# Five tiles of a hybrid attention and recurrence layer turned by VectorE and two DMA passes, in place of TensorE

## The chip, the cores and the metric

The kernel runs on one core of one Trainium2 chip. The metric is the device time of one execution in microseconds (us), the median of several runs. A core has TensorE (PE in the profile; PEld is its weight load), VectorE (DVE), ScalarE (ACT), GpSimd (POOL) and SyncE (SP). Each runs its own instructions in the order in which they were written, and they wait for one another through counting semaphores. The tensors that the engines work on lie in SBUF (128 partitions) or PSUM, the weights and the input in DRAM.

## What is computed

One layer on 256 tokens of width 2048, everything in float32:

```python
h = RMSNorm(x)
hq, hf, hi, hg, c_q, c_kv, k_r = split(h @ w_in)       # 4 x 1024, 512, 512, 64 columns
# head group A: gated linear recurrence, 8 heads of 128, run in two groups (g = 0, 1) of 4 heads
#   f = lb + (1 - lb) * sigmoid(hf);  S_t = diag(f_t) S_{t-1} + (1 - f_t) hi_t^T;  o_t = S_t^T silu(hq_t)
#   o_A = RMSNorm(o) * silu(hg)
# head group B: latent attention, 8 heads
#   q = RMSNorm(c_q) @ w_uq;  k, v = RMSNorm(c_kv) @ w_ukv;  RMSNorm per head, rotary part, softmax
x = x + concat(o_A, o_B) @ w_out
x = x + (silu(g) * u) @ w_down,   g, u = RMSNorm(x) @ w_gate_up
```

## The kernel before, in words

**Products.** Every weight product runs in float32 by parts: a weight tile is split into `w_hi` (ACT, line 757) and `w_lo` (DVE, line 1084), the activations likewise into a `_hi` and a `_lo` tile, and PE adds three products (lines 1693 and 1696). The activations are PE's stationary operand and must stand with the width on the partitions, so each of them is turned (tokens from the partitions to the free axis) before its product.

**Granules.** The first half of the kernel, up to about 430 us, is a row of 137 granules of two weight tiles (128 x 1024 where a block is 512 wide). The blocks stand in this order: `lat` 0 to 2 (the latents `c_q`, `c_kv` and the rotary key), then `hq0 uq0 hf0 ukv0 hi0 uq1 hg0 ukv1 hq1 uq2 ukv2 hf1 uq3 ukv3 hi1 hg1`, then `out1` and `out2`. A block from `w_in` has 8 granules, one from `w_uq` or `w_ukv` has 2. ACT and DVE convert three granules ahead of PE, through a ring of four slots: conversion n waits until PE has used granule n - 4.

**Steps.** Everything else is a step with a place in `SCHEDULE`, which the function `schedule` writes: a granule number and a name. Each engine, in its loop over the granules, first converts (ACT, DVE) or first does its steps and then multiplies (PE). All engines take the steps of a granule in the same order, and no engine passes over one that waits. A conversion that stands behind a waiting or a long step waits with it.

**Turning.** A tile is turned by PE: 8 matmuls of 128 x 128 against `ident`, into a ring of four PSUM banks (`side`), from where ACT and DVE read it. This is so for the normed latents (`lat_t`, `turn_x`, line 1716), the recurrence's queries (`turn` with n = 0, line 1794) and gates (`turn` with n = 1), and the recurrence's output (`o_t`, line 1716). From the feed-forward part on (after 470 us) the kernel has a second way for its hidden tile: DVE turns every 32 x 32 block (line 1475, STREAM_TRANSPOSE), POOL sends the tile to DRAM (line 712) and fetches it back in four pieces in which the blocks have changed places (line 718).

**The steps that the prediction follows.** `q_t` (line 1751) turns the attention's queries, which the step `q_b` makes on DVE (lines 1252 and 1135 to 1140). `lev_b` (lines 1338 and 1339) makes the tiles that `pairs` (line 1805) multiplies. `q_b` also frees the PSUM bank that the block after next needs: the block `hi1` waits for `q_b` of `uq3`.

Of the kernel before, what the change touches and what calls it, by code (L numbers as in the profile page):

```python
# [31 lines left out]
P = 128  # L32
# [182 lines left out]
def schedule():  # L215
# [32 lines left out]
    for g in range(2):  # L248
# [3 lines left out]
        s += [(e + 2 + 2 * g + n * (1 + g), ("turn", g, n, t)) for n in range(2) for t in range(NT)]  # L252
# [10 lines left out]
        s += [(p, ("o_a", g)), (p + 1, ("o_b", g))]  # L263
# [33 lines left out]
def side_uses(step):  # L297

    kind = step[0]
    if kind in ("x", "x2", "lat_t", "o_t"):  # L300
        return [(step, "dve")]
    if kind in ("vec", "turn", "probs_t", "join7", "join8"):
# [24 lines left out]
SPLIT = {step: n for n, step in enumerate(SPLITS)}  # L327

# [31 lines left out]
def hybrid_layer(nc, x, positions, attn_norm_w, w_in, hgrn_lb, hgrn_norm_w, mla_q_norm_w, w_uq, mla_kv_norm_w,  # L360
# [7 lines left out]
    with ExitStack() as ctx:  # L368
# [34 lines left out]
        def mb(name, shape, dt=F32):  # L403
            return sb(name, shape, dt, mix)
# [24 lines left out]
        more_rows = stage[0:V_ROWS - KT, 0, 0, 1, 0:P]  # L429
        keep = mb("keep", [P, SEQ])  # L430
# [15 lines left out]
        latents = (lat, hv)  # L446
        qTn = X[:, 0, :].rearrange("p (h t) -> p h t", h=HEADS)
# [9 lines left out]
        squares = nc.dram_tensor("squares", (P // Q, Q, P // Q, SEQ), F32, kind="Internal").ap()  # L457
        first_two = sb("first_two", [P, WIDE])
# [7 lines left out]
        corner, partly, both = gate[:, 0, :], gate[:, 1, :], hidden[:, 0, :]  # L466

# [45 lines left out]

        s_turned = sem("s_turned")
# [132 lines left out]
        def _(pool):  # L647
# [100 lines left out]
        def _(act):  # L748
# [48 lines left out]

            def split_hi(parts):
# [8 lines left out]
            def step(s):  # L807
# [30 lines left out]
                elif kind == "lat_t":  # L838
                    i, j = a
                    ps, k, col = filled(s), 4 * i + 2 * j, (V_KVN if i else V_QN) + 2 * j  # L840
                    split_hi([(mT_hi[:, k + n, :], ps[:, n * SEQ:(n + 1) * SEQ], col + n) for n in range(2)])
# [46 lines left out]
                elif kind in ("hq", "hf_a", "hi", "hg"):  # L888
# [3 lines left out]
                    if kind == "hq" and not a[0]:  # L892
                        act.wait_ge(s_side, USE[("lat_t", 0, 1)] + 1)
                    if a[0] and kind == "hg":
                        act.wait_ge(s_given["dve"], GIVEN[USE[("o_a", 0, NT - 1)]])
# [3 lines left out]
                elif kind == "turn":  # L899
# [45 lines left out]
                elif kind == "o_t":  # L945
                    g, j = a
                    dst, k = (hT_hi, 12 + 2 * j) if g else (mT_hi, MT[HEADS + 2 * j])
                    split_hi([(dst[:, k:k + 2, :], filled(s)[:, :].rearrange("p (k t) -> p k t", k=2), V_HG)])
# [122 lines left out]
        def _(dve):  # L1071
# [26 lines left out]
            def split_lo(s, parts):  # L1098
# [73 lines left out]
            def step(s):  # L1172
# [33 lines left out]
                elif kind == "lat_t":  # L1206
                    i, j = a
                    ps, k, col = filled(s), 4 * i + 2 * j, (V_KVN if i else V_QN) + 2 * j
                    split_lo(s, [(mT_lo[:, k + n, :], ps[:, n * SEQ:(n + 1) * SEQ], mT_hi[:, k + n, :], col + n)
                                 for n in range(2)])  # L1210
# [98 lines left out]
                elif kind == "lev_a":  # L1309
# [97 lines left out]
                elif kind == "o_t":  # L1407
                    g, j = a
                    hi, lo, k = (hT_hi, hT_lo, 12 + 2 * j) if g else (mT_hi, mT_lo, MT[HEADS + 2 * j])
                    split_lo(s, [(lo[:, k:k + 2, :], filled(s)[:, :].rearrange("p (k t) -> p k t", k=2),  # L1410
                                  hi[:, k:k + 2, :], V_HG)])
# [267 lines left out]
        def _(pe):  # L1679
# [39 lines left out]
            def step(s):  # L1719
# [20 lines left out]
                elif kind == "lat_t":  # L1740
                    i, j = a
                    pe.wait_ge(s_lat, NT * (i + 1))
                    turn_x(s, 2 * j, latents[i])
# [40 lines left out]
                elif kind == "turn":  # L1784
                    g, n, t = a
                    if n == 0:
                        b = BLOCK_OF[("hq", g)]
                        pe.wait_ge(s_taken[b % 2], taken(b))
                    else:
                        pe.wait_ge(s_lbused, g + 1)  # L1790
                    ps = use(s)
                    for h in range(GH):
                        cols = slice(h * P, (h + 1) * P)
                        m = transpose(ps[:, cols], (hq, hlf)[n][:, t, cols], ident[:, :])
# [56 lines left out]
                elif kind == "o_t":  # L1851
# [181 lines left out]
```

## Time and profile before

| | us |
|---|---|
| median of 3 runs | 1124.82 (1124.74 to 1125.54) |
| the profiled execution | 1124.67 |
| its span in the profile | 1122.9 |

The difference between the last two, 1.8 us, lies around the span. The profile gives the busy time of each engine, the waits (who waited for whom), the groups of like instructions, and a timeline, in which each row has the start and the duration of an instruction or of several equal ones in a row, and, in brackets, how long its engine had been idle before it and who ended that. Durations overlap: an engine starts the next instruction before the last one is fully written.

### The profile page before, as it was taken

Reading aid. Unit: us, or ns where it says so; the run is one execution under the profiler, and the core shown is the slowest. Engines: PE = TensorE matmul, PEld = TensorE weight load, DVE = VectorE, ACT = ScalarE, POOL = GpSimd, SP = SyncE. Lnnn points to the kernel's source line nnn. Section 1 sums busy time; section 2 is a strip of 40 time slices with the busy share of each in tenths; the row PEclk is TensorE's granted clock in tenths of the full one; section 3 lists DMA queues with packets and bytes.
Section 4 is the critical chain, followed back from the end, with each engine's and each line's share of the span. In section 5 each row is a group of like instructions: output and inputs, shape, how many; then the busy total and the mean of one; then the engine's idle time right before and its main releaser. Section 6 shows DMA issues by size and latency. Waiting matters only on the chain.

```text
span 1122.9 us, 15465 instructions
## 1 busy us (share of the span) xinstructions
PE 1113.2 (99%) x5265; PEld 937.8 (84%) x5265; DVE 886.8 (79%) x1198; ACT 640.5 (57%) x907; POOL 51.1 (5%) x134
## 2 busy tenths in 40 slices
PE   7999999999999999999999999999999999999998
PEld 7988888888888888888888888888888888888887
DVE  5578786587876667688888888888988879889777
ACT  7566776668664556454554554554554555555553
POOL 3000000000000000000000000000000010000000
PEclk9999999999999999999999999999999999999999
DMA  8666455545555455667777677777777686666655
GB/s 267 192 196 189 158 159 156 164 141 170 197 177 168 153 187 169 212 212 234 225 229 237 222 232 238 222 229 236 224 235 226 224 276 217 207 206 199 211 190 169
DMA packets 107239, 228.99 MB, mean 204 GB/s; under 512 B 8201, under 2 KB 19250, under 8 KB 106930
## 3 DMA queue, kind: packets, MB, share of 16 engines
q1 hardware_dynamic: 101346, 209.30, 58.9%
q0 software_dynamic: 5536, 18.88, 5.8%
q8 instruction: 29, 0.48, 0.2%
q14 instruction: 24, 0.20, 0.0%
q10 hardware_dynamic: 304, 0.14, 0.0%
HBM read 218.32 MB, written 9.96 MB: 203 GB/s over the span
## 4 chain that ended last, share of the span: by engine, by line
PE 97%; DVE 2%; DMA 1%; ACT 0%; issue 0%; SPq 0%; DVEq 0%; ACTq 0%
PE side L1919 25%; PE main L1693 22%; PE side L1921 12%; PE main L1696 11%; PE side L1891 4%; PE side L1892 4%; PE side L1893 4%; PE main L1893 3%; PE main L1891 3%; PE main L1892 3%; PE side L1817 1%; PE side L1716 1%; DMA raw<-in_w_in 1%; PE side L1764 0%; PE side L1765 0%; DVE w_lo L1084 0%
## 5 line engine op out<-in xcount | busy, mean ns | idle before, releaser
L977 ACT CAST w_hi<-raw 128x1024 fp32r<-128x1024 f32 (+1 forms) x245 | 241.6, 990 | 172.2 <-PE side L1919 104.9
L1532 DVE TENSOR_TENSOR w_lo<-raw,w_hi 128x1024 fp32r<-128x1024 f32 (+1 forms) x245 | 275.4, 1139 | 21.9 <-ACT w_hi L977 21.6
L1084 DVE TENSOR_TENSOR w_lo<-raw,w_hi 128x1024 fp32r<-128x1024 f32 (+3 forms) x156 | 178.5, 1154 | 107.9 <-ACT w_hi L757 105.6
L757 ACT CAST w_hi<-raw 128x1024 fp32r<-128x1024 f32 (+3 forms) x156 | 153.7, 993 | 142.5 <-PE main L1693 137.6
L1693 PE MATMUL main<-w_hi,hT_hi 128*128 128x512 f32 (+2 forms) x448 | 173.4, 388 | 1.7 <-DVE hT_lo L1105 1.4
L1696 PE MATMUL main<-w_hi,hT_lo 128*128 128x512 f32 (+2 forms) x448 | 169.1, 378 | 0.0
L1921 PE MATMUL side<-w_hi,hT_lo 128*128 128x512 f32 x400 | 155.6, 389 | 0.0
L1919 PE MATMUL side<-w_hi,hT_hi 128*128 128x512 f32 x400 | 155.6, 389 | 0.0
L1693 PE MATMUL main<-w_lo,hT_hi 128*128 128x512 f32 (+2 forms) x448 | 114.6, 377 | 0.0
L1919 PE MATMUL side<-w_lo,hT_hi 128*128 128x512 f32 x400 | 106.9, 389 | 0.0
L1693 PEld LDWEIGHTS main<-w_hi,hT_hi 128*128 128x128 f32 x448 | 84.7, 189 | 15.5 <-DVE hT_lo L1105 1.8
L1696 PEld LDWEIGHTS main<-w_hi,hT_lo 128*128 128x128 f32 x448 | 84.8, 189 | 13.0
L1693 PEld LDWEIGHTS main<-w_lo,hT_hi 128*128 128x128 f32 x448 | 82.9, 189 | 14.1
L1919 PEld LDWEIGHTS side<-w_hi,hT_hi 128*128 128x128 f32 x400 | 75.1, 188 | 15.6
L1919 PEld LDWEIGHTS side<-w_lo,hT_hi 128*128 128x128 f32 x400 | 75.1, 188 | 15.6
L1921 PEld LDWEIGHTS side<-w_hi,hT_lo 128*128 128x128 f32 x400 | 75.1, 188 | 15.5
L1921 PE MATMUL side<-w_hi,aT_lo 128*128 128x512 f32 x208 | 80.9, 389 | 0.0
L1919 PE MATMUL side<-w_hi,aT_hi 128*128 128x512 f32 x208 | 80.9, 389 | 0.0
L1532 DVE TENSOR_TENSOR w_lo<-last_two,w_hi 128x1024 fp32r<-128x1024 f32 x36 | 44.1, 1225 | 43.5 <-ACT w_hi L977 43.5
L977 ACT CAST w_hi<-last_two 128x1024 fp32r<-128x1024 f32 x36 | 37.9, 1052 | 59.9 <-PE side L1919 59.9
L977 ACT CAST w_hi<-first_two 128x1024 fp32r<-128x1024 f32 x36 | 38.0, 1056 | 58.4 <-PE side L1919 58.4
L1693 PE MATMUL main<-w_hi,mT_hi 128*128 128x512 f32 (+1 forms) x160 | 62.0, 387 | 0.0
(279 smaller groups left out, 1819.0 us busy)
## 6 DMA issues: line engine op xcount, KB each, us to landing
raw<-in_w_gate_up SPq DMA_DIRECT2D x176, 512.0 KB, 4.8
raw<-in_w_down SPq DMA_DIRECT2D x88, 512.0 KB, 4.5
raw<-in_w_in SPq DMA_DIRECT2D x64, 512.0 KB, 3.8
raw<-in_w_out SPq DMA_DIRECT2D x32, 512.0 KB, 3.7
raw<-in_w_in SPq DMA_DIRECT2D x15, 384.0 KB, 4.5
squares<-hiddenT POOLq DMA_DIRECT2D x11, 512.0 KB, 5.0
hiddenT<-squares POOLq DMA_DIRECT2D x44, 128.0 KB, 5.3
raw<-in_w_ukv SPq DMA_DIRECT2D x8, 512.0 KB, 3.9
```

What stands on the lines that cost most here:

```text
L757: copy(w_hi[:, slot, 0:n], raw[:, slot, 0:n]).then_inc(s_hi, 1)
L977: copy(w_hi[:, n % RING, 0:cols], src).then_inc(s_hi, 1)
L1084: tt(w_lo[:, slot, 0:n], raw[:, slot, 0:n], w_hi[:, slot, 0:n].bitcast(F32), ALU.subtract)\
L1532: tt(w_lo[:, n % RING, 0:cols], src, w_hi[:, n % RING, 0:cols].bitcast(F32), ALU.subtract)\
L1693: m = matmul(banks[t][:, 0:cols], hi[:, at[n], tok], rhs, start=(part == "hi" and k == k_first), stop=(part == "lo" and k == last))
L1696: matmul(banks[t][:, 0:cols], lo[:, at[n], tok], rhs, start=False, stop=False)
L1716: m = transpose(ps[:, at:at + P], where[:, t, (k + n) * P:(k + n + 1) * P], ident[:, :])
L1891: matmul(bank, hi, big, start=first, stop=False)
L1892: matmul(bank, lo, big, start=False, stop=False)
L1893: return matmul(bank, hi, small, start=False, stop=last)
L1919: m = matmul(bank, hi, rhs, start=False, stop=(part == "lo" and (t, half) in last))
L1921: matmul(bank, lo, rhs, start=False, stop=False)
```

## The change

Five tiles are turned in the way of the hidden tile: the two normed latents (`lat` 0 and 1), the queries of both recurrence groups (`hq` 0 and 1), and the output of the first group (`o` 0). The gates and the second group's output stay with PE. A new step `swap` does the DVE part, and POOL the moves:

```diff
+            def swap(key, src):                                   # on DVE
+                nc.vector.transpose(swap_of[key].rearrange("p b (n r) -> p n b r", r=Q),
+                                    src.rearrange("p t (k b c) -> p (t k) b c", b=P // Q, c=Q)).then_inc(s_swap, 1)
...
+            def swap(*key):                                       # on POOL
+                n, at = SWAP[key], swap_of[key]
+                pool.wait_ge(s_swap, n + 1)
+                pool.dma_start(swapped[n].rearrange("a c b x -> (a c) b x"), at).then_inc(s_parked, 16)
+                pool.wait_ge(s_parked, 16 * (n + 1))
+                for b in range(P // Q):
+                    pool.dma_start(at[Q * b:Q * (b + 1), :, :], swapped[n, :, :, b, :].rearrange("a c x -> c a x"))\
+                        .then_inc(s_landed, 16)
```

The places in the schedule, and the order on POOL:

```diff
-        s += [(e + 1, ("lat_a", i)), (e + 2, ("lat_b", i))] + [(e + 5, ("lat_t", i, n)) for n in range(2)]
+        s += [(e + 1, ("lat_a", i)), (e + 2, ("lat_b", i)), (e + 2, ("swap", "lat", i))]
+        s += [(e + 13 - 2 * i + n, ("lat_t", i, n)) for n in range(2)]
...
-        s += [(e + 2 + 2 * g + n * (1 + g), ("turn", g, n, t)) for n in range(2) for t in range(NT)]
+        s += [(END[("hq", g)] + 1, ("swap", "hq", g))]
+        s += [(e + 2 - 4 * g, ("turn", g, 0, t)) for t in range(NT)] + [(e + 3 + 3 * g, ("turn", g, 1, t)) for t in range(NT)]
...
-        s += [(p, ("o_a", g)), (p + 1, ("o_b", g))]
+        s += [(p, ("o_a", g)), (p + 1, ("o_b", g))] + [(p + 1, ("swap", "o", g))] * (g == 0)
...
+            swap("lat", 0)
+            swap("lat", 1)
+            swap("hq", 0)
             pool.wait_ge(s_lbused, 1)
             pool.wait_ge(s_side, USE[("join8", 0)] + 1)
             pool.dma_start(lb[:, :, :], hgrn_lb[:, GW:2 * GW].partition_broadcast(P)).then_inc(s_lbin, 16)
+            swap("hq", 1)
+
+            swap("o", 0)
```

ACT and DVE then read the turned tile from SBUF, ACT after a wait for its landing. DVE's split of a latent becomes 4 instructions of 128 x 128 per half in place of 2 of 128 x 256, that of the output 8 of 128 x 128 in place of 2 of 128 x 512:

```diff
-                    ps, k, col = filled(s), 4 * i + 2 * j, (V_KVN if i else V_QN) + 2 * j
-                    split_hi([(mT_hi[:, k + n, :], ps[:, n * SEQ:(n + 1) * SEQ], col + n) for n in range(2)])
+                    k, col = 4 * i + 2 * j, (V_KVN if i else V_QN) + 2 * j
+                    landed("lat", i)
+                    split_hi([(by_quarter(mT_hi[:, k + n, :]), swapped_tile(("lat", i), 2 * j + n), col + n)
+                              for n in range(2)])
```

In granules: `swap` of the latents stands at 19 and 27, their splits at 30, 31 and 36, 37 (before at 22 and 30); `swap` of `hq` at 34 and 74, ACT's copies at 45 and 83 (before at 45 and 89); `swap` of `o` at 81, its split at 95 as before. The swaps write into tiles that are free at the time (`hbT`, `hkT`, half of `E`, the new `hq_turned`, `hgate`).

On PE, between the blocks `ukv0` and `hi0` (line 1693 before is line 1766 now), the rows before:

```order
L1693 MATMUL main<-w_lo,mT_hi 128x512 x4
L1794 MATMUL side<-ident,lat 128x128 x8
L1693 MATMUL main<-w_hi,hT_hi 128x512
L1696 MATMUL main<-w_hi,hT_lo 128x512
L1693 MATMUL main<-w_hi,hT_hi 128x512
```

and now:

```order
L1766 MATMUL main<-w_lo,mT_hi 128x512 x4
L1766 MATMUL main<-w_hi,hT_hi 128x512
L1769 MATMUL main<-w_hi,hT_lo 128x512
L1766 MATMUL main<-w_hi,hT_hi 128x512
L1769 MATMUL main<-w_hi,hT_lo 128x512
```

The 8 matmuls that turned the queries (their tile bears the name `lat`, whose memory it shares) are gone, and the granules on both sides stand next to each other.

On DVE, in front of `q_t` of the first head pair (`stage_r` is what `q_t` turns, `krw` and `kr` the rotary key), the rows before:

```order
L1140 TENSOR_TENSOR kr<-rot 128x2x32
L1084 TENSOR_TENSOR w_lo<-raw,w_hi 128x1024
L1236 TENSOR_SCALAR stat<-stat 128x4
L1084 TENSOR_TENSOR w_lo<-raw,w_hi 128x1024
L1123 TENSOR_TENSOR stat<-stat 128x4
L1124 SCALAR_TENSOR_TENSOR stat<-stat 128x4
```

and now:

```order
L1195 TENSOR_TENSOR kr<-rot 128x2x32
L1164 STREAM_TRANSPOSE E<-lat 128x8x4x32
L1134 TENSOR_TENSOR w_lo<-raw,w_hi 128x1024
L1303 TENSOR_SCALAR stat<-stat 128x4
L1134 TENSOR_TENSOR w_lo<-raw,w_hi 128x1024
L1155 SCALAR_TENSOR_TENSOR mT_lo<-hkT,vec_cols,mT_hi 128x128 x4
L1178 TENSOR_TENSOR stat<-stat 128x4
L1179 SCALAR_TENSOR_TENSOR stat<-stat 128x4
```

A block turn and four small splits have moved in between the rotary key and the work on the queries.

On DVE, behind `q_b` of the third head pair, the rows before:

```order
L1139 TENSOR_TENSOR stage_r<-rot 128x128
L1140 TENSOR_TENSOR stage_r<-rot 128x128
L1084 TENSOR_TENSOR w_lo<-raw,w_hi 128x1024
L1103 TENSOR_TENSOR mT_lo<-side,mT_hi 128x256
L1084 TENSOR_TENSOR w_lo<-raw,w_hi 128x1024
```

and now:

```order
L1194 TENSOR_TENSOR stage_r<-rot 128x4x32
L1195 TENSOR_TENSOR stage_r<-rot 128x4x32
L1164 STREAM_TRANSPOSE hq_turned<-lat 128x8x4x32
L1134 TENSOR_TENSOR w_lo<-raw,w_hi 128x1024
L1153 TENSOR_TENSOR mT_lo<-side,mT_hi 128x256
L1134 TENSOR_TENSOR w_lo<-raw,w_hi 128x1024
```

The turn of the second group's queries stands ahead of the conversion of granule 78. The fifth turn (`hgate<-E`) stands in the same way directly behind the eight instructions of `o_b` (line 1403) and ahead of the conversion of granule 85.

## Rows read from the trace of the kernel before

**Rows 1.** The page, busy time, share and instructions of each engine.

```profile
PE 1113.2 (99%) x5265; PEld 937.8 (84%) x5265; DVE 886.8 (79%) x1198; ACT 640.5 (57%) x907; POOL 51.1 (5%) x134
```

**Rows 2.** Waits of PE, longest first: total us, times, longest.

```profile
PE side L1730 <- POOL freq L669: 3.0, 1, 3.0
PE main L1693 <- DVE hT_lo L1105: 1.4, 2, 1.0
...
```

**Rows 3.** Timeline of PE at the first latent: start, us, instruction.

```profile
54.89 0.75 PE L1693 MATMUL main<-w_lo,hT_hi 128*128 128x320 f32 x4
55.48 1.03 PE L1716 MATMUL side<-ident,lat 128*128 128x128 f32 x8
56.27 0.39 PE L1693 MATMUL main<-w_hi,hT_hi 128*128 128x320 f32 x1
56.50 0.31 PE L1696 MATMUL main<-w_hi,hT_lo 128*128 128x320 f32 x1
```

**Rows 4.** One tile's instructions, `hiddenT`: ns min/median/max, first and last start.

```profile
L718 POOL DMA_DIRECT2D hiddenT<-squares x44: 551/554/570, 478.6 to 904.3; - x44
...
L1475 DVE STREAM_TRANSPOSE hiddenT<-hidden x11: 1233/1235/1240, 471.3 to 895.1; 128x1024 f32<-128x1024 f32 x11
```

**Rows 5.** Groups of DVE and ACT by shape: busy us, mean ns, idle before.

```profile
L1167 DVE SCALAR_TENSOR_TENSOR sincos<-rot,sincos 128x128 f32<-128x128 f32 x6 | 1.8, 292 | 0.2
...
L804 ACT ACTIVATE mT_hi<-side,vec_cols 128x256 fp32r<-128x256 f32 x8 | 3.1, 474 | 0.0
```

**Rows 6.** The page, DMA issues: KB each, median us to landing.

```profile
squares<-hiddenT POOLq DMA_DIRECT2D x11, 512.0 KB, 5.0
hiddenT<-squares POOLq DMA_DIRECT2D x44, 128.0 KB, 5.3
```

**Rows 7.** Timeline of ACT around granules 34 to 36.

```profile
81.44 1.79 ACT L757 CAST w_hi<-raw 128x768 fp32r<-128x768 f32 x2
84.59 1.06 ACT L757 CAST w_hi<-raw 128x1024 fp32r<-128x1024 f32 x1 [1.35 <-PE main L1693]
```

**Rows 8.** Timeline of DVE and PE in front of the first `q_t`.

```profile
90.62 1.23 DVE L1084 TENSOR_TENSOR w_lo<-raw,w_hi 128x1024 fp32r<-128x1024 f32 x1 [2.78 <-ACT w_hi L757]
...
98.65 0.28 DVE L1140 TENSOR_TENSOR stage_r<-rot 128x128 f32<-128x128 f32 x1
...
99.45 0.60 PE L1751 MATMUL side<-ident,stage 128*128 128x128 f32 x4
```

**Rows 9.** Timeline of ACT, DVE and PE up to the first `pairs`.

```profile
111.27 1.05 ACT L757 CAST w_hi<-raw 128x1024 fp32r<-128x1024 f32 x1 [1.67 <-PE main L1693]
...
138.38 1.22 DVE L1339 TENSOR_TENSOR E<-E,hqT 128x1024 f32<-128x1024 f32 x1
...
139.65 1.05 PE L1805 MATMUL side<-E 128*128 128x128 f32 x7
```

**Rows 10.** Timeline of DVE, ACT and PE from granule 78 to granule 89.

```profile
226.56 1.22 DVE L1084 TENSOR_TENSOR w_lo<-raw,w_hi 128x1024 fp32r<-128x1024 f32 x1
...
229.79 0.21 ACT L790 ACTIVATE stat<-stat 128x4 f32<-128x4 f32 x1 [2.47 <-DVE stat L1114]
...
238.65 1.06 ACT L847 ACTIVATE E<-E 128x1024 f32<-128x1024 f32 x1 [2.23 <-DVE E L1222]
...
246.99 0.35 PE L1764 MATMUL side<-X 128*128 128x128 f32 x1 [0.17 <-DVE E L1403]
...
264.15 1.39 DVE L1252 SCALAR_TENSOR_TENSOR stage<-main,stat,qw_row 128x192 f32<-128x192 f32 x4
...
265.64 0.47 PE L1693 MATMUL main<-w_hi,hT_hi 128*128 128x512 f32 x1
```

**Rows 11.** Timeline of DVE and PE at the second group's first `pairs`.

```profile
298.22 1.23 DVE L1338 TENSOR_TENSOR E<-E,hkT 128x1024 f32<-128x1024 f32 x1 [0.28 <-ACT E L920]
299.36 1.22 DVE L1339 TENSOR_TENSOR E<-E,hqT 128x1024 f32<-128x1024 f32 x1
...
301.52 0.50 PE L1805 MATMUL side<-E 128*128 128x128 f32 x3
```

More of the change, by code:

```diff
@@ L299, in side_uses @@
     kind = step[0]
-    if kind in ("x", "x2", "lat_t", "o_t"):
+    if kind in ("x", "x2") or kind == "o_t" and step[1]:
         return [(step, "dve")]
-    if kind in ("vec", "turn", "probs_t", "join7", "join8"):
+    if kind in ("vec", "probs_t", "join7", "join8") or kind == "turn" and step[2]:
         return [(step, "act")]
@@ L891, in step @@
                                "hg": (hgate, ACT.Silu)}[kind]
-                    if kind == "hq" and not a[0]:
-                        act.wait_ge(s_side, USE[("lat_t", 0, 1)] + 1)
+                    if kind == "hq":
+                        act.wait_ge(s_swap, SWAP[("hq", 0) if a[0] else ("lat", 0)] + 1)
                     if a[0] and kind == "hg":
-                        act.wait_ge(s_given["dve"], GIVEN[USE[("o_a", 0, NT - 1)]])
+                        act.wait_ge(s_tlo, SPLIT[("o_t", 0, 1)] + 1)
                     for t in range(NT):
@@ L946, in step @@
                     g, j = a
-                    dst, k = (hT_hi, 12 + 2 * j) if g else (mT_hi, MT[HEADS + 2 * j])
-                    split_hi([(dst[:, k:k + 2, :], filled(s)[:, :].rearrange("p (k t) -> p k t", k=2), V_HG)])
+                    if not g:
+                        landed("o", g)
+                        split_hi([(by_quarter(mT_hi[:, MT[HEADS + 2 * j + n], :]), swapped_tile(("o", g), 2 * j + n), V_HG)
+                                  for n in range(2)])
+                        return
+                    k = 12 + 2 * j
+                    split_hi([(hT_hi[:, k:k + 2, :], filled(s)[:, :].rearrange("p (k t) -> p k t", k=2), V_HG)])
                 elif kind == "sq2":
@@ L1207, in step @@
                     i, j = a
-                    ps, k, col = filled(s), 4 * i + 2 * j, (V_KVN if i else V_QN) + 2 * j
-                    split_lo(s, [(mT_lo[:, k + n, :], ps[:, n * SEQ:(n + 1) * SEQ], mT_hi[:, k + n, :], col + n)
-                                 for n in range(2)])
+                    k, col = 4 * i + 2 * j, (V_KVN if i else V_QN) + 2 * j
+                    split_lo(s, [(by_quarter(mT_lo[:, k + n, :])[:, t, :, :], swapped_tile(("lat", i), 2 * j + n)[:, t, :, :],
+                                  by_quarter(mT_hi[:, k + n, :])[:, t, :, :], col + n) for n in range(2) for t in range(NT)])
+                elif kind == "swap":
+                    what, i = a
+                    if what == "lat":
+                        dve.wait_ge(s_lat, NT * (i + 1))
+                        swap(a, latents[i][:, :, :])
+                    elif what == "hq":
+                        b = BLOCK_OF[a]
+                        dve.wait_ge(s_taken[b % 2], taken(b))
+                        swap(a, hq[:, :, :])
+                    else:
+                        dve.wait_ge(s_given["dve"], GIVEN[USE[("o_a", i, NT - 1)]])
+                        swap(a, E[:, 0, :].rearrange("p (t c) -> p t c", t=NT))
                 elif kind == "kr_b":
@@ L1739, in step @@
                     turn_x(s, 4 * c + 2 * j)
[L1740 to L1743, printed above, removed]
                 elif kind in ("q_t", "k_t"):
@@ L1783, in step @@
                         .then_inc(s_side, 1)
-                elif kind == "turn":
+                elif kind == "turn" and a[1]:
                     g, n, t = a
[L1786 to L1790, printed above, removed]
+                    pe.wait_ge(s_lbused, g + 1)
                     ps = use(s)
@@ L1850, in step @@
                         m.then_inc(s_side, 1)
-                elif kind == "o_t":
+                elif kind == "o_t" and a[0]:
                     g, j = a
```

45 lines of the change are left out of this document (36 added, 9 removed).

## The prediction

> **What bounds the kernel now.** I read the busy shares first: PE is busy for 99% of the span [rows 1]. Then PE's waits: the two longest items are 3.0 us and 1.4 us, both near the start [rows 2]. So PE's own instructions, one behind the other, are the time, and what leaves PE shortens the kernel unless PE then has to wait. Whether it has to can't be seen in shares. For that I read, in the timeline, every place where PE takes up something that DVE or ACT has made, and how much earlier that was ready. There the kernel is tight: the tile of the first `q_t` was written at 98.65 + 0.28 = 98.93 and PE took it at 99.45, 0.52 us later [rows 8]; the first `pairs` got its tile at 138.38 + 1.22 = 139.60 and began at 139.65 [rows 9]; before granule 89 the bank was free at 264.15 + 1.39 = 265.54 and PE wrote to it at 265.64 [rows 10]; before `scores` of the fifth head PE did wait, 0.17 us for DVE [rows 10]. Nearly every reserve of PE is under 1 us there, so PE, DVE and ACT bound this half together, and DVE's work between two such places is on the path.
>
> **What is removed.** PE loses 5 groups of 8 matmuls. One group: it starts at 55.48 and the next granule at 56.27, 0.79 us; that granule's first matmul is followed after 0.23 us (56.27 to 56.50), where four of the same width take 0.59 from 54.89 to 55.48, 0.15 each, so another 0.08 [rows 3]. That is 0.87 us a group and 4.35 us in all. If nothing else happened, the time would be 1124.67 - 4.35 = 1120.3.
>
> **What is added.** DVE gets 5 block turns of 128x1024, and its like takes 1.235 us [rows 4]. An instruction starts about 0.08 us before its predecessor's end (298.22 + 1.23 = 299.45, the next starts at 299.36) [rows 11], so a turn in an unbroken row costs 1.16; behind a wait for its own engine's last write it costs 1.27. The small splits: 4 of 128x128 per half latent. A like of them takes 0.292 [rows 5], 0.21 in a row, so 0.84 us for four. Bounds: 0.14 each, an eighth of the 1.14 us from start to start of a 128x1024 [rows 11], and 0.29 each with no overlap, so 0.6 to 1.2 us for four; I take 0.21, since the row is of the same size and kind. ACT's copies (0.474 each, 0.39 in a row [rows 5]) stay as many, and I take them at the same cost from SBUF. POOL gets 5 stores and 20 loads; one path is 1.24 (turn) + 5.0 (store landed) + 3 x 0.55 (POOL's issues of the first three loads [rows 4]) + 5.3 (last load landed) [rows 6], about 13.2 us. The time from turn to first reader is about 20 us for the latents (swap at 54, split at 75; swap at 72, split at 92), 27 for `hq` 0, over 20 for `hq` 1, 35 for `o`: hidden, at nothing, and with 6 us to spare each.
>
> A rule of the Trainium skill speaks against moving these turns at all: "VectorE: DVE Perf Modes", section "Rules for kernel authors", says that a 128x128 transpose belongs on TensorE where PSUM will do, and the page's table of transpose paths has 390 ns for one there, in bfloat16. By that figure 40 of them would be worth 15.6 us, an estimate; the trace has 0.11 us each in a row [rows 3], and the sum goes by the trace.
>
> **Where the added work lies, place by place.** At each place PE comes at its own pace or when the chain in front of it ends, whichever is later, so waits inside one chain don't add up; only the last counts.
>
> Place 1, up to the first `q_t` (99.45). Two groups are gone before it, 1.74 us. The chain: conversion 36 on ACT was released by PE at 84.59 [rows 7]; 1.74 earlier would be 82.85. But ACT now has two copies (0.78) between conversions 34 and 35, and what leads up to 34 is the rotary angles and their sine table, which moved by the first group alone: 81.44 - 0.87 = 80.57. The conversions 34 and 35 take 1.79 - 0.08 = 1.71 [rows 7], so 36 starts at 80.57 + 1.71 + 0.78 = 83.06, 1.53 earlier than before. Behind it, through `silu` and two table loads, hangs conversion 37, for which DVE waited 2.78 us at 90.62 [rows 8]; so DVE too is 1.53 earlier there. Then it gets the turn of `hq` 0 (+1.16) and four small splits (+0.84) before `q_b`: ready at 98.93 - 1.53 + 1.16 + 0.84 = 99.40. PE would be there at 97.7. It begins at 99.40 in place of 99.45: of 1.74 us, 0.05 is left. (PE stops once earlier, at `uq0`, whose second split now stands at granule 31, for about 0.65 us; the later wait swallows it.) Bounds by the small splits: -0.25 to +0.35 around this.
>
> Place 2, the first `pairs` (139.65). The third group (at 116) is gone. The chain starts at 111.27, where ACT is released by PE [rows 9], and runs through ACT and DVE without another release by PE to 139.60. It moves with PE's place at 111, not with what leaves PE after it. Reserve 0.05, group 0.87: gained 0.05.
>
> Place 3, granules 78 to 89. The chain begins where the fourth turn goes in, ahead of the conversion at 226.56, hands over from DVE to an idle ACT at 229.79 and 238.65, reaches PE with its 0.17 us wait at 246.99 [rows 10], and goes on over the softmax of the fifth head and the gates of the second group, DVE and ACT in turn, to `q_b` of `uq3`, ready at 265.54. PE releases nothing of it. It gets 1.16 (turn of `hq` 1) + 1.27 (turn of `o`, directly behind `o_b`, whose result it reads) = 2.43 us. PE's reserve at the end is 0.10. So granule 89 starts 2.33 us later than before, counted from the same state at 226, and the fourth group, which stood just ahead of it, is inside that: without its removal PE would have come even later, so its gain is nothing. On the way PE should stop several times, at `scores` (the 0.17 us wait becomes longer) and at `probs_t` of the fifth head.
>
> Place 4, from 266 on. The fifth group (at 288) is gone. The next tight place is `pairs` at 301.52, ready at 299.36 + 1.22 = 300.58: reserve 0.94 [rows 11], just over 0.87. DVE's 8 small splits (1.7) stand where 2 large ones with a stop between them took about as long (estimate). So 0.87 is gained. From there on nothing changes.
>
> Sum: -0.05 - 0.05 + 2.33 - 0.87 = +1.4 us. On the profiled execution 1124.67 + 1.4 = 1126.0; the median of the runs stands 0.15 above that execution, so 1126.2.
>
> **Rivals.** (a) The chains give. If the waits in place 3 were not one chain but had slack in them that a timeline doesn't show, or if ACT and DVE catch up, PE keeps its groups: 1120.3 with all hidden (1120.5 as a median); with place 3 alone at nothing the fourth and fifth group count in full, 1124.67 - 0.1 - 1.74 = 1122.8 (1123.0). For it: DVE is idle for a good part of this half, waiting for ACT's conversions. Against it: the idle time lies ahead of conversions that PE releases, not in these chains. Also in this family, one of the two late turns falls into a gap: 1126.2 - 1.2 = 1125.0.
>
> (b) The moves come late. A transfer would have to be 6 us late to delay ACT's split, which waits in order, with all conversions behind it; PE has about 3 us of converted weights, and from there each further microsecond is one on the time. From 9 us late on this is the bound: a path of 25 us at one latent gives 1126.2 + (25 - 13 - 9) = 1129, at both 1132. For it: POOL's moves here run beside the weight loads and beside a busier DVE. Against: such moves took 5.0 and 5.3 [rows 6], also beside weight loads.
>
> The Trainium skill has a mechanism for it: "SBUF — State Buffer", section "SBUF: two separate sides", says that a DMA issued from GpSimd can be held up while DVE holds their shared port. Here that would be held by w_lo's subtractions, 1.22 us long; 25 issues each held for one of them would put 6 us on a path, which is inside the spare time; no run here has yet shown it for these five.
>
> (c) The small splits and the SBUF copies are dearer than taken. At 0.29 a split place 1 costs 0.35 more, the eight splits in place 4 overdraw the 0.07 reserve by 0.6, and longer turns add a little: 1127.3.
>
> **Numbers.** A measurement of this kernel tells a change of about 0.2%, 2.25 us, from none: faster is below 1122.6, slower above 1127.1. The forecast (1125.3 to 1127.1) has 0.52, a partly hidden place 3 (1122.6 to 1125.3) 0.12, the chains give (a, below 1122.6) 0.12, dearer splits (c, 1127.1 to 1128) 0.14, late moves (b, 1128 to 1132) 0.10. Faster 0.12, same 0.64, slower 0.24. The range leaves out most of (a) and (b): 1122.9 to 1128.2.
>
> **What would show it.** Right: 40 fewer matmuls against `ident`; PE's waits grow from about 6 us by some 5 to 6 us, for DVE, at the first `q_t`, the first `pairs`, `scores`, `probs_t` and granule 89; the first `pairs` starts at nearly its old time, 139.5, and granule 89 near 268. Wrong: granule 89 before 266 (then a), ACT waiting for a DMA at a split (b), or a new wait of PE after 301. A DVE turn far from 1.24 us would move place 3 by twice the difference.

## The result, and the profile after

| | before | after |
|---|---|---|
| median of 7 runs each | 1124.86 (1124.74 to 1125.54) | 1129.26 (1128.92 to 1130.74) |
| the profiled execution | 1124.67 | 1129.12 |
| its span | 1122.9 | 1127.4 |

The ratio after / before is 1.0040, 95% interval 1.0029 to 1.0051: slower by 4.4 us, above the range given. The page's row on busy time answers to [rows 1]:

```profile
PE 1112.1 (99%) x5225; PEld 935.8 (83%) x5225; DVE 894.0 (79%) x1217; ACT 642.0 (57%) x909; POOL 64.8 (6%) x159
```

The 40 matmuls are gone from PE. Its waits, which answer to [rows 2]:

```profile
PE side L1803 <- POOL freq L690: 3.0, 1, 3.0
PE main L1766 <- DVE mT_lo L1155: 2.7, 1, 2.7
PE side L1870 <- DVE E L1406: 1.1, 1, 1.1
PE side L1789 <- DMA X<-in_x: 0.9, 1, 0.9
PE main L1766 <- DVE hT_lo L1155: 0.9, 1, 0.9
PE side L1843 <- DVE probs L1356: 0.8, 1, 0.8
PE main L1766 <- issue: 0.8, 1, 0.8
PE side L1833 <- DVE E L1470: 0.6, 1, 0.6
```

The waits at the first `pairs` (L1870), at `scores` and `probs_t` of the fifth head (L1833, L1843) and before granule 89 ("issue") were forecast. The one of 2.7 us for `mT_lo` was forecast at 0.65 and swallowed. It stands before `uq0`; here is PE's timeline there:

```profile
85.31 0.45 PE L1766 MATMUL main<-w_hi,mT_hi 128*128 128x384 f32 x1 [2.65 <-DVE mT_lo L1155]
85.59 0.34 PE L1769 MATMUL main<-w_hi,mT_lo 128*128 128x384 f32 x1
85.77 0.33 PE L1766 MATMUL main<-w_hi,mT_hi 128*128 128x384 f32 x1
...
88.11 0.53 PE L1766 MATMUL main<-w_hi,mT_hi 128*128 128x384 f32 x1
88.43 0.53 PE L1769 MATMUL main<-w_hi,mT_lo 128*128 128x384 f32 x1
...
102.08 0.60 PE L1820 MATMUL side<-ident,stage 128*128 128x128 f32 x4
```

From 88.11 to 88.43 is 0.32 us, from 85.59 to 85.77 only 0.18: matmuls of the same shape stand nearly twice as far apart for a while. The table by stretches (busy time of PE, PEld, DVE, ACT, POOL, then the granted clock, the DMA share and GB/s) names the reason:

```profile
84.00:86.00 2.00, 0.69 (x4) 0.69 (x5) 2.00 (x6) 1.98 (x4) 0.00 (x0) 1.00 0.67 179
86.00:88.00 2.00, 2.00 (x10) 2.00 (x9) 1.97 (x4) 1.99 (x3) 0.00 (x0) 0.69 0.74 243
88.00:90.00 2.00, 2.00 (x7) 2.00 (x7) 1.45 (x2) 1.97 (x3) 0.00 (x0) 0.50 0.72 240
90.00:92.00 2.00, 2.00 (x11) 1.86 (x11) 1.12 (x1) 1.44 (x2) 0.00 (x0) 0.96 0.63 169
```

Behind the stop the granted clock was 0.50, 1.2 GHz in place of 2.4, for about 3.4 us. Before the stop ACT and DVE had this:

```profile
60.45 1.05 ACT L793 CAST w_hi<-raw 128x1024 fp32r<-128x1024 f32 x1 [1.96 <-DMA raw<-in_w_in]
...
68.82 1.05 ACT L793 CAST w_hi<-raw 128x1024 fp32r<-128x1024 f32 x1 [1.23 <-DMA raw<-in_w_in]
...
75.95 0.16 DVE L1201 CAST pos_f<-pos_i 128x2 f32<-128x2 int32 x1
...
81.50 1.13 DVE L1155 SCALAR_TENSOR_TENSOR mT_lo<-hbT,vec_cols,mT_hi 128x128 fp32r<-128x128 f32 x4
...
84.12 1.13 DVE L1155 SCALAR_TENSOR_TENSOR mT_lo<-hbT,vec_cols,mT_hi 128x128 fp32r<-128x128 f32 x4
...
101.08 0.28 DVE L1195 TENSOR_TENSOR stage_r<-rot 128x128 f32<-128x128 f32 x1
```

ACT waits for weights, which it did not before, and the rotary angles (75.95) begin late. The DMA issues between 54 and 68 us, in the kernel after (first the 512 KB loads of `w_in`, then the moves of latent 0; [rows 6] for their like) and, last, in the kernel before:

```profile
raw<-in_w_in SPq DMA_DIRECT2D x6, 512.0 KB, 6.1
swapped<-hbT POOLq DMA_DIRECT2D x1, 512.0 KB, 3.7
hbT<-swapped POOLq DMA_DIRECT2D x4, 128.0 KB, 6.5
...
raw<-in_w_in SPq DMA_DIRECT2D x6, 512.0 KB, 4.5
```

A weight load took 6.1 us to landing in the median, where it took 4.5.

**Where the time went.** The table gives how much later PE starts a step than in the kernel before, read from the timelines of the profiled executions. The executions differ by up to 1.4 us in their first 14 us (the load of `x`), so the difference at granule 16 (44.24 before) is taken off each. The columns: `uq0` (84.33 before), granule 36 (91.28), first `q_t` (99.45), first `pairs` (139.65), granules 89 (265.64), 95 (288.82) and 152 (465.95). In the kernel after nothing changes from 320 us on. Three other profiled executions lose time behind 500 us, where nothing was edited: lat_on_pe 1.8 us, best_a 0.5, best_b 1.1; in lat_on_pe behind a wait of ACT of 4.18 us for weights, in the others the cause was not sought. So compare the places, not the ends.

| kernel | `uq0` | 36 | `q_t` | `pairs` | 89 | 95 | 152 |
|---|---|---|---|---|---|---|---|
| forecast | | | -0.05 | -0.10 | +2.23 | | +1.4 |
| after | +1.03 | +2.68 | +2.68 | +2.76 | +5.18 | +4.19 | +4.61 |
| after, second profile | +1.01 | +2.68 | +2.68 | +2.74 | +5.15 | +4.15 | +4.62 |
| lat_on_pe | 0.00 | 0.00 | +0.66 | +0.76 | +3.16 | +2.14 | +2.55 |
| lat_alone | +1.00 | +2.65 | +2.65 | +2.67 | +2.72 | +2.68 | +2.68 |
| late_alone | 0.00 | 0.00 | 0.00 | +0.02 | +2.44 | +1.43 | +1.90 |
| no_moves | -0.81 | -0.73 | +0.18 | +0.31 | +2.72 | +1.72 | +2.17 |
| stop_2 | +0.31 | +0.39 | +0.38 | +0.45 | +3.14 | +2.14 | +2.57 |
| stop_3 | +0.89 | +2.57 | +2.57 | +2.65 | +5.09 | +4.08 | +4.51 |
| warm | +1.03 | +1.12 | +2.02 | +2.19 | +4.59 | +3.60 | +4.08 |
| angles_early | -1.79 | -1.79 | -0.07 | +0.06 | +2.72 | +1.71 | +2.16 |
| best_a | -1.78 | -1.78 | -0.14 | +0.39 | +0.42 | -0.56 | -0.46 |
| best_b | -1.78 | -1.76 | -1.77 | -1.75 | -1.70 | -2.69 | -2.58 |
| best_c | -1.78 | +5.67 | +5.67 | +5.70 | +5.75 | +4.76 | +4.85 |

The step from `pairs` to granule 89 is +2.42, forecast +2.33. The step up to `q_t` is +2.68, forecast -0.05: there the forecast failed.

### The profile page after: what moved, and what is told of

Its sections match the earlier page's. It is cut to its first block, busy times and chain, and to the rows that moved or that the text cites. A ratio compares the mean times of both kernels' runs of the same rounds, so it can differ in the third digit from the quotient of the medians.

```text
span 1127.4 us, 15411 instructions
## 1 busy us (share of the span) xinstructions
PE 1112.1 (99%) x5225; PEld 935.8 (83%) x5225; DVE 894.0 (79%) x1217; ACT 642.0 (57%) x909; POOL 64.8 (6%) x159
## 4 chain that ended last, share of the span: by engine, by line
PE 90%; DVE 5%; ACT 2%; DMA 1%; issue 1%; POOL 0%; DVEq 0%; ACTq 0%; POOLq 0%; SPq 0%
PE side L1984 24%; PE main L1766 19%; PE side L1986 12%; PE main L1769 9%; PE side L1956 4%; PE side L1958 4%; PE side L1957 4%; PE main L1958 3%; PE main L1957 3%; PE main L1956 3%; DMA raw<-in_w_in 1%; DVE w_lo L1134 1%; PE side L1882 1%; PE side L1789 1%; ACT w_hi L793 1%
```

## The experiments

The theory: POOL's moves of the first latent compete with the weight loads; ACT's conversions come late, and with them the angles; PE stops long before `uq0`; its clock falls behind the stop. Rivals: each turn costs its 0.9 us wherever it stands; VectorE's work alone does it; the late turns do it.

### Which tiles cost what

A tuple names the tiles that PE turns, as in the kernel before; the others stay as in the kernel after.

```diff
+ON_PE = (('lat', 0), ('lat', 1))                    # lat_on_pe
+ON_PE = (('hq', 0), ('hq', 1), ('o', 0))            # lat_alone
+ON_PE = (('hq', 0), ('lat', 0), ('lat', 1))         # late_alone
```

**lat_on_pe.** 

> The two latents are turned by PE again, at their old granules; the three later tiles stay with VectorE. Theory (the excess over the forecast arises at the latents: weight loads late beside POOL's moves, then a stop of PE of 2.65 us before uq0, then a clock at its lower level for about 3.4 us): no stop before uq0 above 0.3 us, granted clock 1.00 from 84 to 92 us, first q_t 0.6 us later than in the kernel before (turn of hq 0 costs 1.16, reserve 0.52), first pairs 0.6 to 0.7 later, granule 89 about 3.0 later, end 2.3 to 2.6 later: 1127.3 us. Rival (each turn costs its 0.9 us wherever it stands, and the clock is no part of it): the first q_t 1 us or more later, and two fifths of 4.4 us gone, 1127.5, with the clock still falling or the 2.6 us not gone at the first q_t. Rival (the late turns alone make the loss): 1129.

Measured 1127.96 (ratio to the kernel before 1.0026, 1.0016 to 1.0037). No stop before `uq0`, `q_t` +0.66, granule 89 +3.16, granule 152 +2.55: the theory's numbers at each place. Its median is 0.7 over the forecast. Its profiled execution was the slowest of the eight (1130.05), 1.8 us of it lost behind 500 us. The times alone do not tell the theory (1127.3) from the first rival (1127.5); the places do.

**lat_alone.** 

> Only the two latents are turned by VectorE and moved by POOL; hq 0, hq 1 and o 0 are turned by PE as in the kernel before. Theory: the same stop of 2.6 to 2.8 us before uq0, the clock at 0.50 for about 3.4 us behind it, first q_t 2.4 to 2.7 us later than in the kernel before, and nothing given back afterwards, since the chains start from PE: end 2.6 later, 1127.4 us. Rival (a late start at 100 us is absorbed by later reserves, or the late turns are what counts): under 1125.8.

Measured 1127.55 (1.0018, 1.0009 to 1.0027); granule 152 at +2.68 in the profile. The stop (2.63 us), the fall of the clock and the 2.65 us are there with the latents alone, and nothing is given back. The profile shows one sort of execution only: of the eleven runs, seven had a mean granted clock of 0.998 or less and took 1127.3 to 1129.4; the other four had 1.000 and took 1125.7 to 1126.1. Six of the seven had 0.998, with a mean of 1127.7, against 1125.8 for the four: where no later wait swallows it, as here, the fall of the clock costs 1.9 us by the runs, 1.65 by the profile.

**late_alone.** 

> Only hq 1 and o 0 are turned by VectorE. Theory (the step of the forecast on granules 78 to 89 was right): granule 89 starts 2.3 to 2.5 us later than in the kernel before, 0.5 to 0.9 is given back at the group removed before granule 95, end 1.5 to 1.9 later: 1126.5 us. Rival (late turns fall into slack once the first half is undisturbed): granule 89 under 1.3 later, 1125.3 or less.

Measured 1126.86 (1.0016, 1.0007 to 1.0025); granule 89 +2.44, granule 152 +1.90. The forecast's step on granules 78 to 89 holds by itself. 2.68 and 1.90 make 4.58 of the 4.61: the turn of `hq` 0 costs nothing in the kernel after, since PE comes to `q_t` later than its tile is ready.

### The moves, or VectorE's work

POOL passes over both latents, and ACT waits for the turn alone:

```diff
+                if key[0] == "lat":
+                    return
                 pool.wait_ge(s_swap, n + 1)
...
-                act.wait_ge(s_landed, MOVED * (SWAP[key] + 1))
+                if key[0] == "lat":
+                    act.wait_ge(s_swap, SWAP[key] + 1)
```

**no_moves.** 

> The kernel after, with POOL's store and four loads of each latent left out (so q, k and v come from tiles whose 32x32 blocks have not changed places); VectorE's turns, the small splits and everything else stay. Theory (the moves delay the weight loads, those delay ACT and with it the rotary angles by about 1 us): ACT's waits for raw at 60, 62 and 69 us are gone, the angles begin 1 us earlier, PE stops before uq0 for 0.9 to 1.7 us in place of 2.65, the clock stays at 1.00, the first q_t comes at 99.6 to 100.3 in place of 102.1, end 1.8 to 2.5 us under the kernel after: 1127.1 us. Rival (VectorE's added work alone does it, the transfers don't matter): stop of 2.5 us, clock falls as before, 1129.2. In between (transfers matter, but the stop is still long enough for the clock): stop of 1.7 to 2.2 and a clock at 0.50 behind it.

Measured 1127.49 (1.0020, 1.0011 to 1.0029), forecast 1127.1. The rows that answer to those of the kernel after:

```profile
60.42 1.05 ACT L795 CAST w_hi<-raw 128x1024 fp32r<-128x1024 f32 x1 [1.09 <-DMA raw<-in_w_in]
...
67.65 1.04 ACT L795 CAST w_hi<-raw 128x1024 fp32r<-128x1024 f32 x1
...
74.94 0.16 DVE L1206 CAST pos_f<-pos_i 128x2 f32<-128x2 int32 x1
...
81.37 0.84 ACT L795 CAST w_hi<-raw 128x768 fp32r<-128x768 f32 x1
...
84.31 0.45 PE L1771 MATMUL main<-w_hi,mT_hi 128*128 128x384 f32 x1 [0.80 <-DVE mT_lo L1160]
...
100.42 0.66 PE L1825 MATMUL side<-ident,stage 128*128 128x128 f32 x4 [0.76 <-DVE stage_r L1200]
```

This execution started 0.84 later than that of the kernel after, so its angles begin at 74.10 on the other's clock, 1.85 us earlier. The stop is 0.80, and PE stops again at `q_t`, as forecast. One wait for weights (1.09) stays, and I can't say why. The forecast's chain is there: with the 0.79 us taken off by which this execution started later than that of the kernel before, conversion 34 starts at 80.58 and 36 at 83.08, where the prediction had 80.57 and 83.06. With the moves left out, `q_t` is at +0.18: all but 0.23 of the missing 2.73 us came from the moves, the fall of the clock that they lead to included.

### The clock

An additional turn, whose result nobody reads, stands ahead of the second split of latent 0, in the kernel without moves. `stop_2` has one of 128x1024, `stop_3` another of 128x512 behind it:

```diff
+                    if (i, j) == (0, 1):
+                        for m, tile in ((2, hq_turned), (1, hqT)):
+                            nc.vector.transpose(tile[:, :, 0:m * P].rearrange("p b (n r) -> p n b r", r=Q),
+                                                hv[:, 0:m, :].rearrange("p t (k b c) -> p (t k) b c", b=P // Q, c=Q))
```

**stop_2.** 

> The kernel without POOL's moves of the latents, with one more turn of 128x1024 on VectorE (a result that nobody reads) ahead of the second split of latent 0. Without it PE stopped 0.97 us before uq0 and its clock stayed at 1.00. Both theories: the stop becomes 2.1 us. Theory (the clock falls after a long enough stop, whatever made the stop): if 2.1 us is long enough, the matmuls of 128x384 behind it stand 0.32 us apart in place of 0.17 for about 3 us, the step after uq0 starts 1.2 to 1.8 us later than the stop alone explains, end 1.8 us over the kernel without moves: 1128.8. Rival (the moves' traffic lowered the clock or slowed the matmuls): spacing 0.17, clock 1.00, first q_t 1.2 us later, end 1128.2.

**stop_3.** 

> As the kernel with one more turn, and half a turn besides (128x512, another 0.6 us). Theory: stop before uq0 of 2.7 us, as in the kernel after, and the clock at 0.50 for 3 to 3.5 us behind it, costing 1.6 us between the starts of granules 33 and 36; first q_t 2.5 to 2.7 us later than in the kernel before (both from the same start), end 1129.3 to 1129.6, although no move of a latent runs. Rival (traffic, not the stop, lowered the clock): clock 1.00, granules 33 to 36 at their old pace, end 1128.8.

PE's timeline of stop_2, then that of stop_3:

```profile
85.08 0.44 PE L1775 MATMUL main<-w_hi,mT_hi 128*128 128x384 f32 x1 [1.93 <-DVE mT_lo L1160]
85.36 0.34 PE L1778 MATMUL main<-w_hi,mT_lo 128*128 128x384 f32 x1
```

```profile
85.47 0.44 PE L1775 MATMUL main<-w_hi,mT_hi 128*128 128x384 f32 x1 [2.52 <-DVE mT_lo L1160]
...
88.54 0.52 PE L1775 MATMUL main<-w_hi,mT_hi 128*128 128x384 f32 x1
88.86 0.52 PE L1778 MATMUL main<-w_hi,mT_lo 128*128 128x384 f32 x1
```

and the stretches of stop_3:

```profile
86.00:88.00 2.00, 2.00 (x10) 2.00 (x9) 1.97 (x4) 1.98 (x3) 0.00 (x0) 0.65 0.23 23
88.00:90.00 2.00, 2.00 (x8) 2.00 (x7) 1.71 (x3) 1.28 (x2) 0.00 (x0) 0.50 0.69 240
```

After a stop of 1.93 us the clock stayed at 1.00 in the profiled execution, and from `uq0` to granule 36 PE lost 0.08. After 2.52 us it fell, and PE lost 1.68, with 23 GB/s of traffic at the fall: the stop does it, not the transfers. (Without the additional turn the stop was the 0.80 shown above, not the 0.97 of the expectation.)

Measured 1129.24 for stop_2 (1.0036, 1.0023 to 1.0049) and 1129.49 for stop_3 (1.0042, 1.0027 to 1.0058). The five runs of stop_2 fall apart: the two with a mean granted clock of 1.000 and 0.999 took 1127.8 and 1127.9, the three with 0.998 took 1129.2 to 1129.9. So at this length the fall comes in some executions and not in others.

Whether it comes goes with the length of the stop in front of `uq0`, but not with it alone. Runs with a mean clock of 0.998 or less: none of 11 without moves (0.80 us), 3 of 5 in stop_2 (1.93), 4 of 4 in stop_3 (2.52), 7 of 11 in lat_alone (2.63), 8 of 12 of the kernel after (2.65). But five kernels whose longest stop behind 20 us was 0.7 to 1.6 us in the profile have such runs too: late_alone, lat_on_pe and best_b one each, angles_early two of ten, best_a three of eleven. And 7 of 75 runs of the kernel before in the batches of the experiments had 0.998, and took 1126.7 to 1127.4 where the others took 1123.9 to 1125.9; none of these was profiled, so where their clock fell is not known.

**after_again.** The kernel after, unchanged. 

> The kernel after, unchanged, beside the others on their chip, for the spread of its runs. Theory (the stop of 2.65 us stands close to the length from which the clock falls, so that most executions have the fall and some may not): runs with a granted clock of 0.998 at 1129.0 to 1129.8, and runs, if any, with 1.00 about 1.7 us below them, 1127.5. Rival (the clock's fall hides behind the later wait and costs nothing): no gap between the two sorts.

Measured 1129.51 (1.0042, 1.0028 to 1.0056). The expected gap of 1.7 us is not there: over both sets, the eight runs at 0.998 have a mean of 1129.73, the four at 1.00 one of 1129.13. The gap is 0.6. In this profiled execution (a stop of 2.64 us) the clock fell as PE resumed, in that of the kernel after 1.45 us later; both lost 1.65 us up to granule 36.

**warm.** PE does something while it waits:

```diff
+                if g == 33:
+                    ps = use(("q_t", 0, 0))
+                    for _ in range(20):
+                        transpose(ps[:, 0:P], ident[:, :], ident[:, :])
                 pe.wait_ge(s_tlo, split_needed(g))
```

> The kernel after, with 20 matmuls of 128x128 (ident against ident, a result that nobody reads) on PE ahead of uq0's wait: they fill 2.2 of the 2.65 us in which PE stood, and are over before the split is ready. Theory (the clock's fall is a cost beside the late conversions): the wait in front of uq0 shrinks to 0.3 to 0.6 us and ends at the same time as in the kernel after, clock 1.00, matmuls of 128x384 0.17 us apart, granule 36 starts 1.65 us earlier than in the kernel after; then PE waits for the first q_t, which VectorE had ready 0.72 us before PE came, so q_t and all behind it come 0.67 us earlier, up to 1.65 if VectorE's work on the queries moves along with PE: end 1128.0 to 1128.9 us. Rival (the slow matmuls behind the stop are no matter of the clock but of late weights): their spacing stays 0.32, end 1129.5. Rival (20 more matmuls cost their time): end 1131.

```profile
82.74 2.34 PE L1941 MATMUL side<-ident 128*128 128x128 f32 x20
85.55 0.45 PE L1766 MATMUL main<-w_hi,mT_hi 128*128 128x384 f32 x1 [0.46 <-DVE mT_lo L1155]
...
87.74 0.33 PE L1766 MATMUL main<-w_hi,mT_hi 128*128 128x384 f32 x1
87.91 0.33 PE L1769 MATMUL main<-w_hi,mT_lo 128*128 128x384 f32 x1
```

Measured 1128.87 (1128.50 to 1128.99, all five with a clock of 1.00; ratio 1.0035, 1.0021 to 1.0049), against 1129.51 for the kernel after in the batch before (the kernel before took 1124.87 and 1124.83 there). The matmuls stand 0.17 apart, granule 36 starts 1.56 earlier, and `q_t` 0.66 earlier: the clock's fall took 1.6 us from PE, of which 0.9 would have been lost at `q_t` anyway, because VectorE had its tile ready only at 101.36. What is left, 0.66, fits the gap of 0.6 in the runs. 20 useless matmuls made the kernel faster by 0.6 us.

### Where a turn is free

**angles_early.** The rotary angles go to where DVE is idle:

```diff
-    s += [(e + 1, ("kr_a",)), (e + 4, ("angles",)), (e + 5, ("sines",)), (e + 9, ("kr_b",))]
+    s += [(e + 1, ("kr_a",)), (11, ("angles", 0)), (13, ("angles", 1)), (14, ("sines",)), (e + 9, ("kr_b",))]
```

> The kernel after, with the rotary angles (VectorE, 4.8 us) in two halves at granules 11 and 13 and their sine table (ScalarE) at 14, in place of granules 29 and 30. Theory (place 1 is lost because that block of work stands between the delayed weights and uq0's splits): no stop before uq0, clock 1.00, the two groups' 1.74 us are kept, so granule 36 starts 1.7 us earlier than in the kernel before and the first q_t at 97.7 to 98.5; first pairs 0.7 to 1.7 earlier than in the kernel before, and place 3 and 4 take 1.9: end 1125.0 to 1126.0 us. Rival (the delayed conversions alone hold PE): the first stop only moves, PE stops for DVE or ACT between granules 26 and 36 for more than 1 us, end over 1127.

Measured 1127.66 (1.0023, 1.0014 to 1.0033), over the expected 1125 to 1126. No stop before `uq0`, and both groups' 1.79 us are in hand at granule 36; but PE then waits 1.57 us for `q_t`, which comes at -0.07. The forecast had been right about what comes last there: VectorE's work from conversion 37 to `q_b`. That its number (-0.05) is nearly met is luck in part: with the angles away this work starts 1.79 us earlier than in the kernel before, not 1.53, and it grew by 2.18 us, not 2.00. My expectation for this run was wrong in forgetting the chain. The profiled execution is the fastest of the ten (1126.51); two of the others, at 0.998, took 1129.1 and 1129.3.

**best_a, best_b, best_c** keep the early angles. In best_a `hq` 0 is turned at granule 38 and `hq` 1 by PE; in the other two PE turns both `hq`. In all three `o` 0 is turned at granule 92, behind the chain that ends at granule 89. The splits of latent 1 stand at 34 and 35, at 39 and 40, and at 32:

```diff
-            s += [(e + 13 - 2 * i + n, ("lat_t", i, n)) for n in range(2)]
+            s += [(e + 13 - 4 * i + n, ("lat_t", i, n)) for n in range(2)]          # best_a
+            s += [(e + 13 + i + n, ("lat_t", i, n)) for n in range(2)]              # best_b
+            s += [(32 if i else e + 13 + n, ("lat_t", i, n)) for n in range(2)]     # best_c
...
+            s += [(END[("hq", g)] + 5, ("swap", "hq", g))]                          # best_a
...
-        s += [(p, ("o_a", g)), (p + 1, ("o_b", g))] + [(p + 1, ("swap", "o", g))] * (g == 0)
+        s += [(p, ("o_a", g)), (p + 1, ("o_b", g))] + [(92, ("swap", "o", g))] * (g == 0 and ("o", 0) not in ON_PE)
...
-        s += [(p, ("o_t", g, 0)), (p, ("o_t", g, 1))]
+        s += [(102 if g == 0 else p, ("o_t", g, 0)), (103 if g == 0 else p, ("o_t", g, 1))]
```

**best_a.** 

> The angles early; the latents by VectorE, the second one split at granules 34 and 35; hq 0 turned by VectorE behind the first q_b (granule 38); hq 1 turned by PE again; o 0 turned by VectorE at granule 92, behind the chain that ends at granule 89, and split at 102 and 103. Theory (a turn costs nothing where it stands behind a chain's end and is split where there is slack): first q_t 1.7 us earlier than in the kernel before, first pairs 1.6 to 1.8 earlier (the third group is swallowed there), granule 89 1.7 earlier, the group of o 0 kept: end 2.0 to 2.7 us under the kernel before, 1122.5 us. Rival (VectorE is full from 96 to 112 us, so hq 0's turn there delays the gates and with them the first pairs): first pairs 0.6 earlier or less, end 1123.5 or more. Rival (any added 1.2 us on VectorE comes back in full): 1125 or more.

Measured 1124.71 (1.0001, 0.9992 to 1.0010), a miss by 2.2. PE waits 1.49 us at `q_t`, where the splits of latent 1 still stand ahead, and 1.4 at the first `pairs`, behind the turn of `hq` 0 (the first rival). Granules 78 to 89 cost 0.03 in place of 2.42, and the group of `o` 0 is kept (-0.98).

**best_b.** 

> Angles early; the two latents by VectorE, the second one split at granules 39 and 40, behind the first q_b; o 0 by VectorE at granule 92, split at 102 and 103; both hq by PE. Theory (a turn costs nothing off the chains): first q_t at 97.7 or up to 0.3 later, first pairs 1.5 to 1.8 earlier than in the kernel before, the same at granule 89, one group more gained at granule 95: end 2.3 to 2.7 under the kernel before, 1122.4 us. Rival (the splits at 39 and 40 delay the gates' reciprocals and with them the first pairs): first pairs less than 1 earlier, end 1123.3 or more.

Measured 1122.50 (0.9977, 0.9968 to 0.9986): faster than the kernel before by 2.3 us, with three of the five tiles turned by VectorE. From `uq0` to 320 us its longest wait is 0.19 us:

```profile
98.20 0.60 PE L1865 MATMUL side<-ident,stage 128*128 128x128 f32 x4
...
138.42 2.05 PE L1919 MATMUL side<-E 128*128 128x128 f32 x16
...
245.81 0.46 PE L1878 MATMUL side<-X 128*128 128x128 f32 x2 [0.19 <-DVE E L1506]
```

**best_c.** 

> As the last, but both splits of latent 1 at granule 32, where VectorE was idle for 3.31 us while ScalarE had its silu. Theory: first q_t at 97.7 to 98.2, end within 0.5 us of the other version, 1122.5. Rival (the later silu delays conversion 36 and PE with it): PE stops before granule 35 or 36 for 0.5 us or more, end 1123 or more.

Measured 1131.01 (1.0057, 1.0043 to 1.0071), 8.5 us over the forecast. The stop and the time lie within the rival's open bounds, but it was not its later `silu` that held the conversions:

```profile
78.03 2.19 POOL L737 DMA_DIRECT2D hkT<-swapped  x4 [2.93 <-DMA swapped<-hkT]
...
87.21 1.70 ACT L853 ACTIVATE mT_hi<-hkT,vec_cols 128x256 fp32r<-128x256 f32 x4 [5.95 <-DMA hkT<-swapped]
...
92.53 0.77 PE L1807 MATMUL main<-w_hi,hT_hi 128*128 128x512 f32 x1 [5.50 <-issue]
```

The turn began at 73.0, so the path took 14.2 us, where the prediction had 13.2. I had put the split where ACT was ready for it 7 us behind the turn's end. ACT waits 5.95 us in order with all conversions behind it, PE stops for 5.50, and the clock falls already in the stop, and for longer than before:

```profile
88.00:90.00 2.00, 0.00 (x0) 0.00 (x0) 1.85 (x8) 1.98 (x5) 0.00 (x0) 0.85 0.00 1
...
92.00:94.00 2.00, 1.47 (x4) 1.23 (x5) 1.40 (x2) 1.97 (x3) 0.00 (x0) 0.50 0.00 0
94.00:96.00 2.00, 2.00 (x6) 1.61 (x5) 1.19 (x2) 2.00 (x4) 0.00 (x0) 0.50 0.65 163
```

## Why the prediction was wrong

**Failed: POOL's path "hidden, at nothing".** The forecast asked whether a move lands in time for its reader. It does: ACT never waits for one in the kernel after. It did not ask what the moves do to others. The store and the four loads of latent 0 run from 55 to 68 us beside the weight loads, and ACT's waits for weights (1.96, 0.34 and 1.23 us at 60 to 69) are the price. The chain of place 1, counted from "81.44 - 0.87 = 80.57", in truth began 1.85 us later. At `q_t` this is 1.84 (warm against no_moves: 2.02 - 0.18). The rival of late moves had the right resource, but on the wrong side of it: it would have the moves as the late ones. The port held by VectorE, named beside it, would also make late moves; no reader waited for one, and POOL's issues for `hbT` took 551 to 570 ns each, as those for `hiddenT` did in the kernel before [rows 4].

**Failed: "PE stops once earlier ... for about 0.65 us; the later wait swallows it".** Without the moves it was 0.80 and was swallowed. With them it was 2.65, and a stop of that length has a price of its own: the clock at 0.50 behind it, 1.65 us on PE, of which 0.66 is on the time. No row of the kernel before showed such a fall, and the forecast had no term for it. In 4 of the 12 runs of the kernel after the mean clock was 1.00, and they too were above the range (1128.9 to 1129.5): the moves' delay alone was enough for the miss.

**Mis-sized: small splits.** Four take 1.05 in a row (0.26 each from start to start; 345 ns from start to end), forecast 0.84, inside the bounds given. That is most of the 0.23 us that are left of the miss at place 1.

**Place 2 (-0.05): +0.08.** The third group is swallowed as forecast; PE waits 1.11 us for `lev_b`.

**Place 3 (+2.33): +2.42 in the kernel after, +2.42 in late_alone.** Both turns (1.24 and 1.25 us) come back whole through chains of DVE and ACT. best_a and best_b lose nothing here. For the turn of `o` 0, which they do behind the chain, that shows that the place was the cost, not the work; the turn of `hq` 1 they give back to PE, so it was not tried at another place. The two turns and the last wait in the kernel after:

```profile
229.29 1.24 DVE L1164 STREAM_TRANSPOSE hq_turned<-lat 128x1024 f32<-128x1024 f32 x1
...
251.77 1.25 DVE L1164 STREAM_TRANSPOSE hgate<-E 128x1024 f32<-128x1024 f32 x1
...
270.77 0.47 PE L1766 MATMUL main<-w_hi,hT_hi 128*128 128x512 f32 x1 [0.78 <-issue]
...
295.07 2.18 DVE L1155 SCALAR_TENSOR_TENSOR mT_lo<-hgate,vec_cols,mT_hi 128x128 fp32r<-128x128 f32 x8
```

**Place 4 (-0.87): -0.57.** The group gives 0.98. Then PE comes to `pairs` before its tile, by too little to be listed as a wait: the eight splits (the last row above) take 2.10 us up to the next instruction, where the two old ones with the stop between them took 1.86, the reserve of 0.94 is overdrawn by 0.98 + 0.24 - 0.94 = 0.28, and 0.42 is lost from granule 95 to granule 152, 0.14 of it not traced. The forecast had "about as long", and named this overdraft only for its rival with dearer splits.

The sum: -0.05 - 0.05 + 2.33 - 0.87 gave +1.4; measured +2.68 + 0.08 + 2.42 - 0.57 = +4.61. Of the 3.2 us between them 1.84 is the moves' delay of the weights, 0.66 the clock, 0.23 the splits at place 1 and 0.3 at place 4; the rest is place 2 and 3.

**Open.** What in the transfers delays the weights (the number of packets, the queue, DRAM) was not tried. Nor is it known what decides in which executions the clock falls. Neither is it known why the load of `x` at the start differs by up to 1.4 us between profiled executions.

## What to carry to other kernels

A transfer that is in time for its own reader is not yet free: look up which loads run beside it, and how far their reader is from waiting. Where PE is the bound, count a stop of about 2 us or more at more than its length, since the clock may fall behind it (here in 3 of 5 runs at 1.93 us, in 19 of 27 at 2.52 to 2.65). Look at the clock of all runs, not only of the profiled one. And a step's cost is that of its place: look for the end of the chain that runs through it, and put it behind.

## What the hardware showed

A stop of PE of 1.93 us left the granted clock at 1.00 in the profiled execution (with other executions of the same kernel at 0.998). Stops of 2.52, 2.63, 2.64 and 2.65 us were each followed in the profiled execution by some 3.4 us at 0.50, which began between 0 and 1.5 us after PE resumed. In one of 5.50 us (best_c) the clock fell during the stop and came back 3.7 us after its end. Matmuls on `ident` in the gap kept it at 1.00 (warm). The fp32 turn of 128x1024 took 1.24 to 1.25 us on VectorE on all five tiles. The 512 KB weight loads beside the store and the four loads of latent 0 took 6.1 us to landing in the median, against 4.5 in the kernel before and 5.1 with the moves left out; a split of 128x128 from SBUF took 0.345 us from start to end and 0.26 from start to start in a row.
